# PEER tables of the sample tokens as dense streamed matrices, in a kernel that gathered rows for every token

## The reference

```python
q = (xt @ wq).reshape(T, PEER_HEADS, 2, PEER_HALF)          # 8 heads
s1 = einsum('thd,hnd->thn', q[:, :, 0], k1)                 # 128 scores
s2 = einsum('thd,hnd->thn', q[:, :, 1], k2)                 # 128 scores
v1, i1 = top_k(s1, 16);  v2, i2 = top_k(s2, 16)
cand = v1[..., :, None] + v2[..., None, :]                  # 256 sums
cid = i1[..., :, None] * 128 + i2[..., None, :]
sc, pos = top_k(cand, 16)
eid = take_along_axis(cid, pos);  gate = softmax(sc)
ub = take(u_tab, eid);  act = gelu(einsum('td,thkd->thk', xb, ub))
vb = take(v_tab, eid);  out = einsum('thk,thkd->td', gate * act, vb)
```

## Time and profile before

| | us |
|---|---|
| timed runs, median of 3 | 3021.3 |
| lowest and highest | 3018.28 and 3039.55 |
| profiled execution, span from its first to its last instruction | 2689.4 |
| median less that span | 331.9 |
| share of the span: PE / DVE / POOL / ACT busy | 80% / 61% / 56% / 19% |
| bytes read from HBM | 909 MB |

### The profile page before, as it was taken

How to read it: one execution, slowest core, us unless ns; L and a number is a source line. 1 busy time by engine, 2 the same in 40 slices (tenths; PEclk the granted TensorE clock), 3 DMA queues, 4 the chain that set the end, 5 groups by cost and what they waited for, 6 DMA issues and landing times.

```text
span 2689.4 us, 25633 instructions
## 1 busy us (share of the span) xinstructions
PE 2146.1 (80%) x6324; PEld 1057.5 (39%) x6324; DVE 1636.2 (61%) x3913; ACT 510.5 (19%) x1291; POOL 1514.9 (56%) x1543
## 2 busy tenths in 40 slices
PE   6999695967878786776899996777777777777777
PEld 2555442423333333332447653333333333333333
DVE  3224568677676675767433436767667675767665
ACT  2160211111111111121242122111111211111112
POOL 0000377777777777677500006777777676767774
PEclk9999797989888898887989997888888888888889
DMA  9984499999999999999723118999999999999996
GB/s 294 313 259 163 169 407 403 407 410 407 410 400 410 407 410 396 410 408 409 303 68 95 59 35 321 407 381 398 399 405 389 383 408 396 393 393 382 410 409 255
DMA packets 326341, 912.92 MB, mean 339 GB/s; under 512 B 31952, under 2 KB 128464, under 8 KB 325744
## 3 DMA queue, kind: packets, MB, share of 16 engines
q0 software_dynamic: 221184, 805.40, 75.9%
q1 hardware_dynamic: 97840, 101.20, 11.6%
q10 hardware_dynamic: 7232, 5.39, 0.7%
HBM read 909.26 MB, written 2.63 MB: 339 GB/s over the span
## 4 chain that ended last, share of the span: by engine, by line
PE 38%; issue 21%; DMA 17%; DVE 12%; POOL 9%; ACT 1%; ACTq 1%; POOLq 1%; DVEq 0%
PE psum L727 16%; DMA arena<-in_peer_u,idx 16%; PE psum L670 9%; POOL arena L326 6%; POOL arena L332 4%; PE psum L708 3%; PE psum L635 3%; PE psum L849 2%; DVE arena L1086 1%; PE psum L657 1%; PE psum L927 1%; PE psum L788 1%; DVE i12u L1034 1%; DVE small L1052 1%; ACTq L362 1%
## 5 line engine op out<-in xcount | busy, mean ns | idle before, releaser
L727 PE MATMUL psum<-arena,diag 128*128 128x512 f32 x3072 | 1409.8, 621 | 476.4 <-ACT diag L467 476.4
L326 POOL DMA_INDIRECT arena<-in_peer_u,idx x768 | 762.1, 992 | 908.1 <-issue 520.8
L1086 DVE SCALAR_TENSOR_TENSOR arena<-arena,xtok 128x1024 f32<-128x1024 f32 x768 | 940.6, 1225 | 539.4 <-DMA arena<-in_peer_u,idx 510.4
L727 PEld LDWEIGHTS psum<-arena,diag 128*128 128x128 f32 x3072 | 609.1, 200 | 1266.7 <-issue 817.7
L332 POOL DMA_INDIRECT arena<-in_peer_v,idx x768 | 748.8, 975 | 234.2 <-issue 228.7
L467 ACT ACTIVATE diag<-ident,wts 128x128 f32<-128x128 f32 x768 | 270.2, 394 | 534.2 <-PE psum L727 499.3
L670 PE MATMUL psum<-arena,slab 128*128 128x384 f32 x672 | 226.1, 494 | 6.9 <-DMA slab<-in_rg_w_out 4.7
L670 PEld LDWEIGHTS psum<-arena,slab 128*128 128x128 f32 x672 | 127.6, 192 | 99.8 <-issue 11.5
L708 PE MATMUL psum<-area 128*128 128x384 f32 (+1 forms) x512 | 160.9, 473 | 0.0
L461 ACT ACTIVATE tanh<-inner 128x16 f32<-128x16 f32 (+2 forms) x52 | 11.1, 213 | 676.6 <-DVE inner L1093 676.5
L708 PEld LDWEIGHTS psum<-area 128*128 128x128 f32 x512 | 97.2, 190 | 63.9 <-issue 6.7
(11 more groups left out here) (205 smaller groups left out, 1389.7 us busy)
## 6 DMA issues: line engine op xcount, KB each, us to landing
slab<-in_ada_w SPq DMA_DIRECT2D x33, 1024.0 KB, 8.3
area<-in_peer_wq SPq DMA_DIRECT2D x16, 1024.0 KB, 16.5
arena<-in_peer_u,idx POOLq DMA_INDIRECT x768, 7.8
arena<-in_peer_v,idx POOLq DMA_INDIRECT x768, 7.9
slab<-in_gla_w_in SPq DMA_DIRECT2D x12, 1024.0 KB, 5.4
keys<-in_ada_w SPq DMA_DIRECT2D x8, 1024.0 KB, 7.8
area<-in_ada_w SPq DMA_DIRECT2D x7, 1024.0 KB, 8.7
slab<-in_rg_w_in SPq DMA_DIRECT2D x5, 1024.0 KB, 11.5
```

Of the source, the lines that this page charges most:

```text
L326: pool.indirect_dma_start(ubuf[j % US], None, u_rows, bass.IndirectOffsetOnAxis(ap=idx[t][:, j:j + 1], axis=0)).then_inc(u_in[j % US], 16)
L727: mm = pe.matmul(acc[t][:, half * 512:(half + 1) * 512], diag[j % DS][:, :], vbuf[j][:, half * 512:(half + 1) * 512], start=False, stop=Tr ...
L1086: dve.scalar_tensor_tensor(ubuf[j % US], ubuf[j % US], 1.0, xtok[:, t * D:(t + 1) * D], ALU.mult, ALU.mult, accum_out=dots[t][:, j:j + 1]) ...
```

## The change

The prompt tile (128 tokens) keeps gathering. The two sample tiles (256 tokens) no longer gather: both tables are streamed whole as matmul weights.

1. **U sweep.** A new input `peer_ut` holds `peer_u` transposed, in 128 tiles of 128 experts. SP streams them (512 KB each, ring `tab` of 4). PE multiplies each tile by the 256 sample tokens: 8 matmuls of 256 columns (`experts`). ACT writes the GELU of the result to `S`, 128 experts x 128 tiles x 256 tokens, the whole of the new buffer `big` (16 MB). Queries and scores of the 8 heads are woven into the first 16 pairs of tiles (`U_PLAN`), for all three token tiles at once.
2. **Routing** on DVE (`choose`) works on groups of 2 or 4 heads; only the 54 sums that can be among the top 16 are formed, and a one-hot of 16 x 54 picks the row number.
3. **Gates.** After the U sweep, row numbers and gates of the sample tokens are transposed (`turn`). For each token, DVE writes two one-hot matrices over its 128 choices (`pairs`) and PE multiplies them (`gates`): the product is the gate of each of the 16,384 experts for that token. DVE multiplies it into `S` (`weigh`), four tokens at a time. The prompt tile's first 96 slots go into the same stretch on PE (`prompt`), 3 for every 2 groups.
4. **V sweep.** SP streams `peer_v` in 128 tiles; PE multiplies each by `S` (`sample`), 8 matmuls of 256 columns into 4 PSUM banks. The last 32 slots of the prompt go between tiles from tile 61 on.
5. `S` takes the room of the input `xT`, query weights and keys: `xT` is written to HBM (`x_keep`) and read back, keys and query weights are loaded only after the norm's statistics, gather rings have 3 buffers for U and 3 for V, and the weight slabs of GLA are loaded only after the V sweep of layer 0.

All loops are unrolled. The core of the diff:

```diff
+def experts(k):                                                # PE, U sweep
+    if k >= 2:
+        pe.wait_ge(sem("tu_ev"), PAIRS * layer + k - 1)
+    for i in (2 * k, 2 * k + 1):
+        wait_table(i)
+        for c in range(C):
+            mm = pe.matmul(bank[k % 2][:, (i % 2) * TS:(i % 2 + 1) * TS],
+                           tab[i % TABS][:, c * P:(c + 1) * P], hP[:, c, TP:T], ...)
+        mm.then_inc(sem("tab_used"), 1)
...
+def gates(g):
+    pe.wait_ge(sem("pair_ready"), n + 1)
+    if g >= 4:
+        pe.wait_ge(sem("w_done"), n - 3)
+    for j in range(GRP):
+        mm = pe.matmul(bank[g % 4][:, j * NK:(j + 1) * NK], onehots[:, g % 3, j, 1, :],
+                       onehots[:, g % 3, j, 0, :], start=True, stop=True)
...
+def prompt(s):
+    pe.wait_ge(v_in[n % RING], 16 * (n // RING + 1))
+    pe.wait_ge(sem("diag_ready"), n + 1)
+    for half in range(2):
+        mm = pe.matmul(acc[:, half * 512:(half + 1) * 512], diag[n % 4],
+                       vbuf[n % RING][:, half * 512:(half + 1) * 512], ...)
...
+def sample(i):                                                 # PE, V sweep
+    wait_table(NTAB + i)
+    for c in range(C):
+        mm = pe.matmul(out_s[c], tab[i % TABS][:, c * P:(c + 1) * P], S[:, i, :], ...)
...
+for g in range(NG):                                            # NG = 64
+    gates(g)
+    for s in range(3 * g // 2, 3 * (g + 1) // 2):
+        prompt(s)
...
+def pairs(g):                                                  # DVE
+    for j in range(GRP):                                       # GRP = 4
+        k = GRP * g + j
+        dve.tensor_scalar(onehots[:, g % 3, j, 0, :], iota[:, :], i1T[:, k:k + 1], gT[:, k:k + 1],
+                          ALU.is_equal, ALU.mult)
+        ins = dve.tensor_scalar(onehots[:, g % 3, j, 1, :], iota[:, :], i2T[:, k:k + 1], None,
+                                ALU.is_equal)
+def weigh(g):
+    dve.wait_ge(sem("g_pe"), NG * layer + g + 1)
+    w = S[:, :, GRP * g:GRP * (g + 1)].rearrange("p i j -> p j i")
+    dve.tensor_tensor(w, bank[g % 4].rearrange("p (j i) -> p j i", j=GRP), w, ALU.mult)
...
+def table(i):                                                  # SP
+    if i >= TABS:
+        sp.wait_ge(sem("tab_used"), 2 * NTAB * layer + i - TABS + 1)
+    if i < NTAB:
+        src = peer_ut[layer, i]
+    else:
+        src = peer_v[layer, (i - NTAB) * P:(i - NTAB + 1) * P, :]
+    sp.dma_start(tab[i % TABS], src).then_inc(tab_in[i % TABS], 16)
...
+pool.wait_ge(sem("x_kept"), 16 * (layer + 1))                  # POOL, prompt tile only
+up(layer, range(0, 48))
+down(layer, range(0, 3))
+up(layer, range(48, PART + 3))                                 # PART = 96
+down(layer, range(3, PART + 3))
+up(layer, range(PART + 3, HK))                                 # HK = 128
+down(layer, range(PART + 3, HK))
```

More of the change, by code:

```diff
@@ L219, in build @@
             sem(n) for n in ("vec_in", "const_in", "x_in", "pos_in", "bd_in", "gla_small_in", "mask_in", "s0_in"))
-        keys_in, wq_in = sem("keys_in"), sem("wq_in")
+        keys_in = sem("keys_in")
+        wq_in = [sem(f"wq_in{i}") for i in range(2)]
         SEG = [(0, TP), (TP, T)]
-        def apart(eng):
-            eng.sem_inc(sem("waited"), 1)
-        def parts(last, t):
-            return LAST_PARTS if last and t == NT - 1 else (range(TOPK),)
         block = ctx.enter_context(nc.Block())
@@ new lines, in peer @@
+                queries(0)
+                sp.wait_ge(sem("xn_ready"), 4 * (n + 1))
+                sp.dma_start(x_keep, xflat).then_inc(sem("x_kept"), 16)
+                sp.wait_ge(sem("h_ready"), 16 * (n + 1))
+                queries(1)
+                for i in range(TABS):
+                    table(i)
+                done = TABS
+                for h in range(2, PH):
+                    queries(h)
+                    for i in range(done, 4 * h - 2):
+                        table(i)
+                    done = max(done, 4 * h - 2)
@@ new lines, in peer @@
+                for i in range(2 * layer):
+                    act.wait_ge(sem(f"st_gla_out{i}"), 16 * HEADS)
+                for step, i in U_PLAN:
+                    if step == "q":
+                        queries(i)
+                    elif step == "s":
+                        scores(i)
+                    elif step == "x":
+                        prompt_tokens()
+                    else:
+                        if i == EXP_PAIR:
+                            exps()
+                        experts(i)
@@ L736, in peer @@
-                pe.wait_ge(keys_in, 16 * (layer + 1))
-                first_tile()
-                pe.wait_ge(sem("first_s_ev"), 2 * (layer + 1))
-                pe.wait_ge(sem("h_ready"), 32 * (layer + 1))
-                routing(layer)
-                queries(0, 1)
-                scores(0, 1)
-                pe.wait_ge(sem("xt_ev"), 6 * (layer + 1))
-                for t in range(NT):
-                    for half in range(2):
-                        pe.matmul(acc[t][:, half * 512:(half + 1) * 512], zrow[0:1, :],
-                                  zrow[0:1, 0:1].to_broadcast([1, 512]), start=True, stop=True, skip_group_check=True)
@@ L761, in peer @@
[L761 to L762 removed]
+                            if h == 0 and half == 0:
+                                pe.wait_ge(sem("h_ready"), 16 * (2 * layer + 1) + 2 * c + 2)
+                            mm = pe.matmul(bank[6 + half][:, 0:T], wq[h % 2][:, c, half * P:(half + 1) * P],
+                                           hP[:, c, :], start=(c == 0), stop=(c == C - 1))
+                        mm.then_inc(sem("q_mm"), 1)
@@ new lines, in scores @@
+                def scores(h):
+                    if h == 0:
+                        pe.wait_ge(keys_in, 16 * (layer + 1))
+                    else:
+                        pe.wait_ge(sem("s_ev"), 2 * (PH * layer + h))
+                    for half in range(2):
+                        pe.wait_ge(sem("q_ev"), 2 * (PH * layer + h) + half + 1)
+                        o = (2 * h + half) * NK
+                        for t in range(NT):
+                            mm = pe.matmul(bank[2 + half][:, t * NK:(t + 1) * NK], qT[half][:, t * P:(t + 1) * P],
+                                           pkeys[:, o:o + NK], start=True, stop=True)
+                        mm.then_inc(sem("s_mm"), 1)
@@ new lines, in peer @@
+                for step, i in U_PLAN:
+                    if step == "q":
+                        queries(i)
+                    elif step == "s":
+                        scores(i)
+                    elif step == "x":
+                        prompt_tokens()
+                    else:
+                        experts(i)
+                turn()
+                pe.wait_ge(sem("xt_ev"), 2 * (layer + 1))
+                zero(bank[4])
+                zero(bank[5])
+                pe.wait_ge(sem("tu_ev"), PAIRS * (layer + 1))
```

708 lines of the change are left out of this document (377 added, 331 removed).

## The result

| | median us | lowest to highest | runs |
|---|---|---|---|
| before | 3030.4 | 3018.3 to 3047.6 | 4 |
| changed | 3147.8 | 3147.1 to 3148.5 | 4 |

The change makes the kernel slower by 3.8%: ratio 1.0379 [1.0335, 1.0423]. The forecast was 3496 us, slower by 16%, with a range from 3265 us.

The account below looks back on a forecast made before the run. PE was taken to bound the changed kernel: 1283.7 us of work a layer, 1294.9 with seams, lengthening the span from 2689.4 to 3164 us; plus 332 outside it, 3496 us. Own range 3430 to 3560, with rivals 3265 to 3620.

Parts of the forecast that it names:

- The step that failed: Whole program: the 331.9 us between profiled span and timed median taken as a constant, added to 3164 us.
- Rival 2: Time outside the span: it grows with the run, as if timed executions ran everything slower; 3554 us, chance 0.15.
- PE's sum: PEER, one layer: all matmul work on PE adds up to 1283.7 us, of which the two sweeps are 887.
- The seam after the U sweep: Between U sweep and first gates: last GELU, two copies and first one-hots take about 5 us a layer.
- Table tiles: Both sweeps: a streamed tile lands within the 10.4 us its slot allows, so PE loses nothing.
- Clock: PE in PEER: granted clock 1.00, its level of 2.4 GHz.
- Prompt rows: Gates' stretch: gathered V rows land in 4.2 to 5 us, within the 5.5 us left, so nothing is lost.
- rival 3: Gates' stretch not PE's: V rows landing in 7.9 us, 3665 us; or stepped product costing 2.8 us, 3600 us; chance 0.15.
- DVE in the gates' stretch: Gates' stretch: DVE needs 2.4 us a group, with the stepped product at 0.69 us, under PE's 3.65.
- Routing: DVE beside the U sweep: done between 446 and 537 us after PEER begins, before the sweep's end at about 541.
- The first: Time outside the span: it belongs to the gathers and shrinks with their number, 1536 to 512; 3275 us, chance 0.17.
- fourth: Both sweeps: matmuls overlap on PE, so 887 us a layer would halve; 2609 us, chance 0.04.

Follow-up runs that it names:

- usual execution: Kernel before, unchanged, timed and profiled again: 3076.2 us, ratio 1.0054; its profiled execution took 3063.6 us, with a span of 3061.7 us.
- quick execution: Kernel before, unchanged, in the first profile on which the prediction rests: span 2689.4 us; its own time is not on record.

## Why the prediction was wrong, and where it was right

**The step that failed** is "the median of the runs lies 331.9 us above that ... If it is a constant around the program". It isn't around the program: only 1.8 to 2 us are, in every run whose span is on record. The 332 us were time inside PEER, mostly waits (372 us in the usual execution that was profiled), and absent from the quick one. The changed kernel has 1.9 us around its span, and none of its 1530 starts in the routing is late but six that wait for scores. The sum itself needed no offset: its rows are of PE's work and of the parts outside PEER, and these last took 574.5 us in the quick execution and 574.8 us in the usual one: 3164 + 2 = 3166 us would then have been the forecast, 0.6% off, and 3166 / 3030 = 1.045. What stood against it was in view: a range of 21 us over three runs, and one profile 11% below all of them. I listed this extra as belonging to the gathers, to the run's length or to neither. Rival 2 had timed executions run slower, but all of their work alike and in the changed kernel too; that the profiled execution itself was the exception was not among the rivals.

**PE's sum: right.** From first query to last V record, layer 0 took 1575.7 - 291.3 = 1284.4 us; 1283.7 + 10 was forecast. Queries and U sweep 542.5 us; PE's terms for them are 542.2. Gates' stretch 240.5; 234, some 3.7 of zeroing and 3 of seam. V sweep to 1575.7, 501.3; 499.6. The seam after the U sweep cost 1.1 us instead of 5, and the small waits hid too; that is the 9 us a layer.

**Table tiles: right.** 1.3 us were waited in all, and DMA at 195 to 242 GB/s in PEER; 217 was forecast. **Clock: right**, 1.00.

**Prompt rows: right.** 10.8 us of waits on V rows over both layers; the 170 us that rival 3 had for a landing in 7.9 us did not come.

**DVE in the gates' stretch: right in effect, wrong in size.** The stepped product took 1.29 us, 1.9 times the 0.69 assumed, and below the 2.8 at which I had put the rival. The eight scalar operations start 0.23 us apart, so a group is some 3.1 us, still under PE's 3.7. The Trainium skill, "SBUF — State Buffer", section on the DMA port swizzle, says that accesses that leave a 16-byte line pay a penalty; the trace agrees, at 1.9 times, against a row whose two inputs both lie in SBUF in order (`weigh` takes one from PSUM; what that is worth by itself no run shows).

**Routing: right.** DVE had idled for 41 us when the last softmax reached it, so its part was done 493 us after PEER began, between the 446 and 537 forecast; the 864-element operations took 1.06 us, as worked out. The row in the changed kernel's timeline:

```profile
818.71 0.29 DVE L1202 TENSOR_REDUCE ztop<-gate_p 128x8 f32<-128x128 f32 x1 [40.97 <-ACT gate_p L494]
```

**Rivals.** None gives 3148 us. The first was nearest in what it said (the extra belongs to the gathers) and not in its price: with a third of the gathers left all of it went, not two thirds. Why none of it is left is not shown; DMA moves 195 to 242 GB/s in the changed kernel's PEER, far from full. The second, third and fourth are refuted by the span, by rows 833.88 to 1074.40 above, and by 0.217 us a record. The Trainium skill's issue gap ("TensorE: Matmul & The Clock Gate", "Back-to-back issue gap") would have made a record 0.195 us by my estimate from it; the trace disagrees.

**Where a gain went.** The bytes fell from 913 to 652 MB and the DMA over the whole span from 298 GB/s in the usual execution to 207, and the time rose. The gathered V matmuls of the sample's two tiles took 2 x 128 x 4 records of 0.437 us a layer, 448 us, and the V sweep puts 444 us in their place. The U sweep is 444 us of PE where DVE had done the dot products beside it.

## What stays open

Why chained instructions start late. It goes with how gathers are issued (gone at four under way or at a longer pause, back at five) and with full DMA engines, and neither is enough by itself: with the longer pause 2 of 383 starts after full DMA are late, in the quick execution none of 791. It is not the loops, the increments or the rows read. It does not look like a block by the gather on POOL: a start was 5.21 us late across four gathers with 0.3 us between them, 31 of the 133 late gaps have no instruction on POOL at all, and of the 99, 53% begin under a gather on POOL, against 51% of the other gaps. The Trainium skill, "SBUF — State Buffer", section "Who interferes with whom", has VectorE and GpSimd exclude each other only where VectorE reads two SBUF inputs or is in a mode with two ports; the start that was 5.21 us late is a top-8 with one input, so the rule as told does not cover it. Nor is it shown why the quick execution had none with gathers as dense. The packets' own records differ there too: of those of 4 KB, 0.6% took over 250 ns in the quick execution and 3.5% in the usual one (3.5% with the pause, 4.2% with the longer one, 6.4% with four under way, where late starts are gone). So such packets are not what makes starts late, and no version here gets rid of them; whether they are the reason that none comes near 2689 us is untested.

Where the gain of the pause comes from. That it is the late starts is a guess: without the increments, and with a pause after U rows only, 1.5% came with 89 and 81 of them, and POOL waits longer for row numbers with the pause (659 us) than without (562). What makes up the part of the 372 us beyond the 217 us of `choose` is open as well.

## What to carry to other kernels

Before an offset between the runs' time and a profile's span is added to anything, ask whether a profiled execution's own time is that far off too: here it was 2 us, and the rest was an execution that did not happen again. A sum over the bounding engine's records, each priced by a row of the same shape, held to 0.6% of a span. To swap gathers for dense sweeps, count the matmul records first: in float32 a sweep of 128 tiles over 256 tokens costs 444 us of PE whatever the number of rows wanted. And where DMAs are issued as fast as they will go, try issuing them a little slower: a fill of 0.22 us after each gather, 0.09 us more from gather to gather, gained 2.7%.

## What the hardware showed unexpectedly

- DVE instructions that wait for DVE's own semaphore up to 5.2 us late, 181 us in an execution, nearly all of them while DMA moved some 400 GB/s; with the same DMA rate in another execution, none.
- Gathers of 512 KB need at least five under way: three gave 269 GB/s, four 325, five to eight 336 to 348.
- A DVE product of 512 elements with steps of 1 KB in SBUF, the other input from PSUM: 1.29 us instead of 0.69.
